# GpSimd makes the weights' low halves in pieces of 256 columns, and a gate's product in two

## What is computed

```
x = x + 0.5 * rms_norm(swiglu(rms_norm(x), ffn1_w_gu) @ ffn1_w_down)        # "f1", 2816 hidden
x = x + rms_norm(mixer(rms_norm(x)) @ w_o)                                  # LRU scan and window attention
x = x + 0.5 * rms_norm(swiglu(rms_norm(x), ffn2_w_gu) @ ffn2_w_down)        # "f2"
for i in (0, 1):                                                            # second block, 256 context tokens beside
    m = silu(c) @ ada_w[i] + ada_b[i]                                       # "ada": shifts, scales and gates
    h = layer_norm(a*h + m[2] * mixer_i(h*(1+m[1]) + m[0]))                 # 0: retention, 1: neighbourhood attention
    h = layer_norm(a*h + m[5] * swiglu_2(h*(1+m[4]) + m[3]))                # "f3", "f4", 2816 hidden
```

## Time and profile before

| | |
|---|---|
| median of 3 runs | 2793.99 us (2793.39 to 2797.36) |
| the profiled execution | 2799.06 us, span 2797.2 us |
| TensorE matmul (PE) | 99% of the span |
| VectorE (DVE) | 68% |
| ScalarE (ACT) | 44% |
| GpSimd (POOL) | 14% |
| granted TensorE clock, mean | 0.998 of full |

### The profile page before, as it was taken

One profiled execution on the slowest core, in us unless ns is written; L12 is line 12 of the kernel. 1 busy time (PEld: TensorE's weight loads), 2 busy tenths in 40 slices (PEclk: granted clock), 3 DMA queues, 4 the chain that ended last, 5 costly groups with the idle time before them and its releaser, 6 DMA issues.

```text
span 2797.2 us, 42563 instructions
## 1 busy us (share of the span) xinstructions
PE 2766.6 (99%) x16554; PEld 2459.0 (88%) x16554; DVE 1893.6 (68%) x3430; ACT 1237.3 (44%) x2248; POOL 402.0 (14%) x219
## 2 busy tenths in 40 slices
PE   9999999999999999999999999999999999999998
PEld 8888896988888888888888999999997787989898
DVE  7788788858895653444435896666686636778686
ACT  5332358642233552332314653344355546545353
POOL 2243300023332011011011000000001323000000
PEclk9999999999999999999999999999999999999999
DMA  6565512236554211111011112222223121222322
GB/s 204 184 189 188 166 64 83 84 104 221 188 191 134 77 54 61 38 61 61 31 61 50 43 54 82 61 68 72 72 76 102 50 76 54 75 83 91 106 91 83
DMA packets 86024, 267.91 MB, mean 96 GB/s; under 512 B 9152, under 2 KB 18752, under 8 KB 85568
## 3 DMA queue, kind: packets, MB, share of 16 engines
q1 hardware_dynamic: 85824, 265.20, 29.6%
HBM read 261.49 MB, written 2.10 MB: 94 GB/s over the span
## 4 chain that ended last, share of the span: by engine, by line
PE 87%; DVE 7%; DMA 3%; ACT 2%; issue 2%; SPq 0%; DVEq 0%; ACTq 0%
PE ps L2072 27%; PE ps L2073 27%; PE ps L2074 27%; DMA t_raw<-in_gu 2%; DVE t_wlo L2764 2%; PE ps L2351 1%; PE ps L2335 1%; PE ps L2324 1%; ACT t_whi L2394 1%; DMA t_x<-in_x 0%; PE ps L2216 0%; DMA t_raw<-in_dn 0%; PE ps L2208 0%; DVE t_raw L2773 0%; PE ps L2267 0%
## 5 line engine op out<-in xcount | busy, mean ns | idle before, releaser
L2072 PE MATMUL ps<-t_h,t_whi 128*128 128x512 f32 (+2 forms) x2152 | 727.3, 338 | 5.0 <-DVE t_wlo L2755 1.9
L2073 PE MATMUL ps<-t_h,t_wlo 128*128 128x512 f32 (+2 forms) x2152 | 721.3, 335 | 0.0
L2074 PE MATMUL ps<-t_h,t_whi 128*128 128x512 f32 (+2 forms) x2152 | 721.1, 335 | 0.0
L2394 ACT CAST t_whi<-t_raw 128x1024 fp32r<-128x1024 f32 (+3 forms) x449 | 368.4, 830 | 565.7 <-PE ps L2074 369.4
L2072 PEld LDWEIGHTS ps<-t_h,t_whi 128*128 128x128 f32 x2152 | 408.3, 190 | 50.3 <-issue 9.9
L2073 PEld LDWEIGHTS ps<-t_h,t_wlo 128*128 128x128 f32 x2152 | 408.5, 190 | 36.5 <-issue 1.2
L2074 PEld LDWEIGHTS ps<-t_h,t_whi 128*128 128x128 f32 x2152 | 408.3, 190 | 35.4
L2072 PE MATMUL ps<-t_hid,t_whi 128*128 128x256 f32 (+2 forms) x1320 | 428.4, 325 | 1.9 <-DVE t_hid L3058 1.7
L2073 PE MATMUL ps<-t_hid,t_wlo 128*128 128x256 f32 (+2 forms) x1320 | 426.1, 323 | 0.0
L2074 PE MATMUL ps<-t_hid,t_whi 128*128 128x256 f32 (+2 forms) x1320 | 425.5, 322 | 0.0
L2764 DVE TENSOR_TENSOR t_wlo<-t_raw,t_whi 128x512 fp32r<-128x512 f32 (+3 forms) x360 | 321.4, 902 | 106.9 <-ACT t_whi L2394 104.0
(11 more groups left out here) (355 smaller groups left out, 4840.6 us busy)
## 6 DMA issues: line engine op xcount, KB each, us to landing
t_raw<-in_gu SPq DMA_DIRECT2D x174, 512.0 KB, 3.4
t_raw<-in_ada SPq DMA_DIRECT2D x96, 512.0 KB, 3.6
t_raw<-in_dn SPq DMA_DIRECT2D x52, 512.0 KB, 4.2
t_raw<-in_dn SPq DMA_DIRECT2D x24, 384.0 KB, 3.4
t_raw<-in_ret_v SPq DMA_DIRECT2D x16, 512.0 KB, 3.5
t_raw<-in_ret_qk SPq DMA_DIRECT2D x16, 512.0 KB, 3.3
t_raw<-in_ret_g SPq DMA_DIRECT2D x16, 512.0 KB, 3.4
t_raw<-in_ret_o SPq DMA_DIRECT2D x16, 512.0 KB, 3.8
```

Of the source, the lines that this page charges most:

```text
L2072: e.matmul(out, whi, xlo, start=first, stop=False, skip_group_check=shared)
L2073: e.matmul(out, wlo, xhi, start=False, stop=False, skip_group_check=shared)
L2074: return e.matmul(out, whi, xhi, start=False, stop=last, skip_group_check=shared)
L2394: e.copy(m.block(0, it.slot, n), m.raw(it)).then_inc(*S["hi"].of(j))
```

## The change

GpSimd's low half of a block becomes four instructions of 256 columns (three for a block of 768); a block that lies in a slot with a third dimension is cut along that dimension, in pieces of 256 or 512. Only the last piece raises the semaphore. A gate's product of 512 columns becomes two instructions of 256.

```diff
@@ prep_lo and gate of gpsimd_program @@
             w.wait_ge(f"d_ring{it.raw % NR}", it.raw)
             w.wait_ge("hi", j)
-            e.tensor_tensor(m.block(1, it.slot, n), m.raw(it), m.block(0, it.slot, n), ALU.subtract).then_inc(*S["lo_pool"].of(j))
+            lo, raw, hi = m.block(1, it.slot, n), m.raw(it), m.block(0, it.slot, n)
+            for o in range(lo.shape[1]) if len(lo.shape) == 3 else range(0, n, 256):
+                some = o if len(lo.shape) == 3 else slice(o, min(o + 256, n))
+                done = e.tensor_tensor(lo[:, some], raw[:, some], hi[:, some], ALU.subtract)
+            done.then_inc(*S["lo_pool"].of(j))
...
-            e.tensor_tensor(s, s, m.rs(it.t0, it.n), ALU.mult).then_inc(
-                *S["gate_pool"].of(it.key, *((it.f, "rs", h) for h in halves(it.t0, it.n))))
+            rs = m.rs(it.t0, it.n)
+            for o in range(0, it.n, 256):
+                done = e.tensor_tensor(s[:, o:o + 256], s[:, o:o + 256], rs[:, o:o + 256], ALU.mult)
+            done.then_inc(*S["gate_pool"].of(it.key, *((it.f, "rs", h) for h in halves(it.t0, it.n))))
```

## The result

| | before | after |
|---|---|---|
| median | 2795.68 us (2793.39 to 2799.17, 4 runs) | 2827.68 us (2824.60 to 2831.71, 4 runs) |
| the profiled execution | 2799.06 us, span 2797.2 | 2824.60 us, span 2822.8 |

The ratio is 1.0119, 95% interval 1.0107 to 1.0131: 32 us slower. The prediction said 2801.3, and 2812 at most.

What follows compares the result with a forecast made beforehand. TensorE was taken as the bound, matmuls filling 99% of the span. Terms -3.2 + 4.8 + 1.7 + 4.0 = +7.3 us gave 2806.4 profiled; less 5.1, a median of 2801.3 us, range 2789 to 2812.

Steps and rivals of the forecast that it cites:

- The first net's ring has the same rounds, with weights made much further ahead; there I count 0: First feed-forward: delays in its raw-buffer rounds cost 0, at worst a few us.
- The ring in f2: Second feed-forward's raw buffers: each gate ends 1.0 us later over six rounds; +4.0, between -3.9 and +6.0.
- The retention, +4.8: Near 1082, 1246 and 1409 us: VectorE's turn delays GpSimd's low half, TensorE idles 1.6 us three times.
- one fall of the clock, +1.7: In the retention: TensorE's clock falls behind one of the three waits, +1.7 us.
- At 30 us, -3.2: VectorE gets in earlier, saving 1.5 of TensorE's 1.9 us wait and a 1.7 us clock loss; between 0 and -3.6.
- near enough what one gate's product of 512 costs alone: Price of the gate's split: two pieces of 256 columns take 1.4 us, about the same as the whole.
- The planner within 2 us: Fourth rival, chance 0.05: the planner's reordering decides, with the time within 2 us of before.
- The upper end, 2812: Top of the forecast range: all three falls of the clock in the retention and the full 6.0 in f2.
- The 5.1 between the two: The profiled execution of before stood 5.1 us above the median, taken off to forecast the median.
- The rivals: Ring absorbs it, 0.22; shorter VectorE waits speed f2's end, 0.15; pieces keep VectorE out, 0.08; planner's moves decide, 0.05.
- The pieces did not stay together: Third rival, chance 0.08: four pieces shut VectorE out for 2.83 us like one instruction; +2 to +5 us.
- The signs: Expected in the profile after, among others: no VectorE instruction of lines 3010 or 3058 longer by more than about 0.7 us.

Runs made afterwards that it cites:

- lows_f1: Against before, low halves in pieces in the first feed-forward alone (fourth GpSimd low half to 340 us), products whole: 2804.93 us, ratio 1.0041.
- lows_f2: Against before, low halves in pieces in the second feed-forward alone (566 to 875 us), products whole: 2811.64 us, ratio 1.0062.
- before_short_mul: Before, low halves and products whole, with the modulation's multiplies on VectorE cut to 128 of 1024 columns: 2793.57 us, ratio 0.9997.
- lows_from_retention: Against before, low halves in pieces only in the retention stage and behind it (from about 900 us): 2799.80 us, ratio 1.0020.
- whole_new_order: Against before, the planner is shown the pieces, so the order is after's, but the chip gets whole instructions: 2796.36 us, ratio 1.0009.
- lows_first3: Against before, only the first three low halves of GpSimd in pieces (up to 34 us): 2793.87 us, ratio 0.9997.

## Why the prediction was wrong

- **"The first net's ring has the same rounds, with weights made much further ahead; there I count 0".** This is the first step that failed: `lows_f1` measured +11 us. Two things were wrong in it. The weights were far enough ahead there, but the hidden parts, which come out of the same chain, were 4.5, 1.5 and 0.4 us ahead of TensorE, and I had not read them. And a lag in the ring is not paid once against the stock, it adds up from round to round; in nine rounds it was 10 us.
- **The ring in f2, "+4.0", with a bound of +6.0.** This is the second, and the larger in us. The mechanism was right, the term was mis-sized: `lows_f2` measured +17. The forecast looked for the loss in the rounds up to 861 us and at the end of f2. In after 11.5 us were lost before that, between 647 and 747, where the weights ran out, and none from 770 to 861, where a round with the same blocks took 12.0 us against the 11.8 of before. The round of the earlier trace rows was put together with VectorE waiting at one border in a low half, since there a multiply happened to come late. In the stage from 94 to 202 us four pieces took 5.1 us in the mean. Each turn of VectorE adds about 1.0 (1.71 less 0.74), so that is a little over two turns and not one; the hold grew by 2.6 us and not by 1.6. I also counted only the gate's delay (1.0) as the loss of a round and took the longer hold of the raw buffer as hardly felt by the next load, "which is hardly moved". Even the first two rounds behind 94 us, in which there is no gate, took 11.2 and 11.1 us in after against 9.4 and 9.2 in before: the hold alone makes a round 1.9 us longer.
- **The retention, +4.8 and one fall of the clock, +1.7.** Three waits at the forecast places, by the forecast mechanism, 1.4 us each in place of 1.6: +4.2. The clock fell behind none of them. The run with this part alone, +6, is near the 6.5 in sum by luck, since it holds no fall of the clock.
- **At 30 us, -3.2.** The wait fell by 1.3 where 1.5 was forecast, and the clock stayed up; in the traces 2.1 us were gained by 41 us, because TensorE then waited 0.4 us for another product (line 2944, at 36 us), which the forecast had not looked for. The fall at 33 us does not come each time: of the seven traces with whole low halves there (waits of 1.6 to 2.1 us) three have it, before, `before_short_mul` and `lows_from_retention`, and four have not; of the six with pieces (0.8 at most) none has. `whole_new_order` gained 1.6 us there with no split at all. `lows_first3`, the run with this part alone, shows no gain that can be told.
- **The gate's product in two, "near enough what one gate's product of 512 costs alone".** Costed at nothing, measured +6 with an interval of 3 to 9; the traces put it at the hidden parts at 336 and 868 us.
- **The planner within 2 us**: +2 (-0.3 to +5), which does not speak against it.
- **The sums.** The upper end, 2812, is said to be all three falls of the clock and the full 6.0. These give 12.7 us, 2811.8 on the profiled execution, but 2806.7 for the median. The 5.1 between the two was read from three runs; with the four of the result it was 3.4. And it may take off twice what a fall of the clock at 33 us had cost in the one execution that was read. None of this reaches 2827.7.
- **The rivals.** All of them lay within 10 us of before or below it. What came true, that the ring falls behind TensorE and the hidden parts with it, was in the prediction only as the mild half of a term. The pieces did not stay together: a median piece of 1712 ns is one that has waited for a turn of VectorE. What was drawn from the Trainium skill (GPSIMD Engine Reference, 2.1 Instruction dispatch), that four pieces could keep VectorE out, did not come true either: the longest multiply between 94 and 202 us took 1758 ns. The Trainium skill's page "SBUF — State Buffer" (🔬 SBUF: two separate sides) says that whichever engine has the shared ports keeps them for the whole instruction. The traces agree (a hidden part took 2.69 us beside a whole low half), and show that at the end of it the other one is next.
- **The signs.** On VectorE's side the forecast held: in the whole of after no instruction of line 3010 took over 1.76 us and none of line 3058 over 1.22, where before had up to 3.47 and 2.88.

## What to carry to other kernels

Cutting an instruction into pieces to let a rival engine in gives that engine a turn at every border, and the price is set by the length of that engine's instructions, not by the piece: 0.70 us of work became 1.7. Before a step in a ring is made longer, compare the pace of the ring with that of the engine it feeds, round by round, and read the margin at every product of the chain: at the hidden parts at the end of the stage, which were the tightest in f1, and at the blocks of weights in its middle, which ran out in f2. A price that keeps the ring within the pace of that engine was nearly free here, and one above it added up over the rounds.

## What the runs showed of the hardware

- GpSimd and VectorE take turns at the borders of instructions: with multiplies of 1.2 us on VectorE, the pieces of 256 columns last 1712 ns in the median and 1821 at most, and 742 in the median when the multiplies are cut to 128 columns.
- A lone wait of TensorE of 1.1 us for its weights, three times, left the clock at 2.4 GHz; in the wait of 4.9 us it fell, and was at 1.2 GHz for 6.8 us.
- A fall of the clock of 3.4 us at 33 us, which cost some 1.6 us, was in three traces behind waits of 1.9 to 2.1 us, and missing in four behind waits of 1.6 to 1.9. The same wait of 1.9 us brought one in before and none in `whole_new_order`. So one trace does not tell whether a stall of that length brings a fall.
